# Weight loads sorted by the event that frees each buffer, a new order of expert steps, and the front part in the same Block

## What is computed

```python
xn = rmsnorm(h, g_mix); proj = xn @ w_in            # q, k, v, compressed and selected keys, gates
y_a = dilated_attention(...); y_b = nsa_attention(...)
merged = sigmoid(g_a) * (y_a @ w_branch_a) + sigmoid(g_b) * (y_b @ w_branch_b)
h = h + merged @ w_out
h = h + moe_ffn(rmsnorm(h, g_ffn))                  # 64 experts, top 8 per token, and a shared expert
h = h + (p @ w_ple) * sigmoid(rmsnorm(h, g_ple) @ w_ple_gate)
out = rmsnorm(h, g_final)
```

## Time and profile before

| | us |
|---|---|
| median of 3 runs (1224.35 to 1226.53) | 1225.8 |
| the profiled execution | 1225.4 |
| its span, first to last instruction | 1223.6 |
| PE busy | 1124.3 (92%) |
| DVE / ACT / POOL busy | 474.1 / 275.7 / 284.8 |
| mean share of the 16 DMA engines, whole span | 65% |
| DMA in all | 306.20 MB, mean 250 GB/s |

### The profile page before, as it was taken

The page is one execution under the profiler, slowest core; times in us unless marked ns, Lnnn a source line. Parts: engine busy times, 40 slices in busy tenths (PEclk is TensorE's granted clock), DMA queues, the critical chain, the costliest instruction groups (busy, mean ns, idle before and its releaser), DMA issues.

```text
span 1223.6 us, 19017 instructions
## 1 busy us (share of the span) xinstructions
PE 1124.3 (92%) x7561; PEld 657.0 (54%) x7562; DVE 474.1 (39%) x1044; ACT 275.7 (23%) x634; POOL 284.8 (23%) x212
## 2 busy tenths in 40 slices
PE   4999999999997989988999998989899897989796
PEld 3887787767765879554433343334333343323274
DVE  5335555545445743553225211212111121111786
ACT  3113333333335320010111111111111111111623
POOL 5532534343233430000111111111111111110032
PEclk8999999999997989979999998999999999989898
DMA  9821222211113203647689999999999999999771
GB/s 281 236 69 36 55 68 70 53 52 53 53 53 121 86 28 121 282 178 323 254 304 424 423 424 412 418 412 423 396 413 421 388 424 404 402 424 359 292 309 69
DMA packets 118040, 306.20 MB, mean 250 GB/s; under 512 B 21792, under 2 KB 79808, under 8 KB 91968
## 3 DMA queue, kind: packets, MB, share of 16 engines
q1 hardware_dynamic: 105712, 270.88, 57.9%
q0 software_dynamic: 12240, 34.09, 7.0%
HBM read 289.21 MB, written 26.21 MB: 258 GB/s over the span
## 4 chain that ended last, share of the span: by engine, by line
PE 37%; DMA 20%; issue 6%; SPq 2%; DVE 1%; POOLq 1%; POOL 1%; ACT 0%; DVEq 0%
DMA sb_gate_up<-in_w_up 20%; PE bank L1431 15%; PE bank L1455 7%; PE bank L1055 4%; PE bank L1043 4%; PE bank L1080 2%; PE bank L1421 2%; PE bank L1024 1%; SPq L971 1%; DMA sb_xg<-xn_rows,sb_work 1%; PE bank L1074 1%; POOLq L1782 1%; POOL sb_small L1785 1%; SPq L1471 1%; PE bank L928 0%
## 5 line engine op out<-in xcount | busy, mean ns | idle before, releaser
L1431 PE MATMUL bank<-sb_gate_up,sb_xgT 128*32 128x512 f32 (+2 forms) x2144 | 312.9, 621 | 35.8 <-DMA sb_gate_up<-in_w_up 35.8
L1431 PEld LDWEIGHTS bank<-sb_gate_up,sb_xgT 128*32 128x32 f32 (+2 forms) x2144 | 99.2, 121 | 217.9 <-issue 215.1
L457 PE MATMUL bank<-sb_x_hl,sb_w_hl 128*128 128x512 f32 x768 | 201.3, 406 | 0.0
L457 PEld LDWEIGHTS bank<-sb_x_hl,sb_w_hl 128*128 128x128 f32 x768 | 138.6, 190 | 43.8 <-issue 16.0
L1504 POOL DMA_INDIRECT expert_rows<-sb_rows_out,sb_work x42 | 43.2, 1029 | 479.7 <-DVE sb_rows_out L1576 459.9
L1455 PE MATMUL bank<-sb_down,sb_work 128*32 128x512 f32 (+2 forms) x1072 | 153.0, 595 | 1.5 <-ACT sb_work L1628 0.6
L241 POOL TENSOR_TENSOR sb_w_hl<-sb_r,sb_w_hl 128x1024 fp32r<-128x1024 f32 x54 | 132.0, 2449 | 65.6 <-ACT sb_w_hl L1163 52.9
L1586 DVE TENSOR_TENSOR sb_work<-sb_work,bank 128x256 f32<-128x256 f32 x42 | 17.8, 423 | 300.1 <-ACT sb_work L1622 300.1
L1622 ACT ACTIVATE sb_work<-bank 128x256 f32<-128x256 f32 x42 | 16.2, 386 | 327.4 <-PE bank L1431 327.4
L1455 PEld LDWEIGHTS bank<-sb_down,sb_work 128*32 128x32 f32 (+2 forms) x1072 | 47.2, 116 | 75.7 <-issue 71.9
L235 POOL CAST sb_w_hl<-sb_r 128x1024 fp32r<-128x1024 f32 x35 | 37.7, 1077 | 205.5 <-PE bank L457 158.1
(11 more groups left out here) (250 smaller groups left out, 1270.6 us busy)
## 6 DMA issues: line engine op xcount, KB each, us to landing
sb_gate_up<-in_w_gate SPq DMA_DIRECT2D x64, 1024.0 KB, 17.1
sb_gate_up<-in_w_up SPq DMA_DIRECT2D x64, 1024.0 KB, 24.0
sb_down<-in_w_down SPq DMA_DIRECT2D x64, 1024.0 KB, 21.3
sb_r<-in_w_in SPq DMA_DIRECT2D x34, 512.0 KB, 3.9
sb_rows<-expert_rows SPq DMA_DIRECT2D x6, 2048.0 KB, 16.2
sb_r<-in_w_out SPq DMA_DIRECT2D x8, 512.0 KB, 3.7
sb_rows<-expert_rows SPq DMA_DIRECT2D x4, 1024.0 KB, 7.8
sb_h<-in_x SPq DMA_DIRECT2D x4, 512.0 KB, 8.2
```

Of the source, the lines that this page charges most:

```text
L457: last = nc.tensor.matmul(out[:, :], w6_hl[:, slot_at[n], zw, k, :], x_hl[:, zx, k, :], start=k + i == 0, stop=k == KD - 1 and i == 2)
L1431: last = nc.tensor.matmul(bank[BH][rows, :], xgT[:, k, rows], gate_up[slot_of[r]][:, :, k, :], start=k == 0, stop=k == KD - 1)
```

## The change

The functions of the front become `front_sync`, `front_gpsimd`, `front_tensor`, `front_vector` and `front_scalar`, unchanged inside, and are called at the head of the second Block; the first Block is gone. ACT gets one wait ahead of the sigmoids. The order of steps is written as a string of units. The loads of the weights go to the buffer that is free first, and SP's list of loads is sorted by the event that frees the part they go to. The buffers that the tail uses are named by the last six experts instead of by fixed numbers.

```diff
-        with nc.Block() as block:
-            @block.sync
-            def _(sp):
+        def front_sync(sp):
...
-        steps = [full(r) for r in range(NPRE)]
-        next_small = NFULL + 2 * NTRIO
-        pairs_at, full_at = (0, 2, 4, 5, 7, 9, 11, 12), {3: 3, 6: 4, 10: 5}
-        for g in range(NTRIO):
-            if g in pairs_at:
+        UNITS = "FPFPFTPTTPTFTPTTPTFTPTTPTFTT"
+        steps, n_full, n_trio, next_small = [], 0, 0, NFULL + 2 * NTRIO
+        for u in UNITS:
+            if u == "F":
+                steps.append(full(n_full))
+                n_full += 1
+            elif u == "P":
                 steps.append(pair_of(next_small, next_small + 1))
                 next_small += 2
-            if g in full_at:
-                steps.append(full(full_at[g]))
-            steps += trio(NFULL + 2 * g, NFULL + 2 * g + 1, next_small)
+            else:
+                steps += trio(NFULL + 2 * n_trio, NFULL + 2 * n_trio + 1, next_small)
+                n_trio += 1
...
-        nth = {r: x for x, r in enumerate(ranks_in_order)}
-        slot_of = {r: nth[r] % NSLOT for r in ranks_in_order}
-        landed_at = {r: 16 * (nth[r] // NSLOT) + 16 for r in ranks_in_order}
+        load_order = list(range(NPRE)) + sorted((r for r in first_step if r >= NPRE), key=lambda r: (first_step[r], steps[first_step[r]].index([v for v in steps[first_step[r]] if v[0] == r][0])))
+        BUFFER = 1,2,0,3,4,5
+        slot_of, landed_at, before, holder = {}, {}, {}, {}
+        for x, r in enumerate(load_order):
+            v = x if x < NSLOT else min(holder, key=lambda i: (last_step[holder[i]], i))
+            if v in holder:
+                before[r] = holder[v]
+            landed_at[r] = 16 + (landed_at[before[r]] if r in before else 0)
+            slot_of[r], holder[v] = BUFFER[v], r
+        loads = sorted([(last_step[before[r]], 0, x, "gate_up") for x, r in enumerate(load_order) if r in before]
+                       + [(last_step[before[r]] + 1, 1, x, "down") for x, r in enumerate(load_order) if r in before])
...
             round_piece(WM_PIECE + 5)
+            act.wait_ge(F["evicted"], NF)
             for m in range(4):
                 gate(m)
...
         def experts_sync(sp):
...
+            sp.wait_ge(M["stored"], 16 * NT)
+            sp.wait_ge(M["xt_done"], NT)
+            sp.wait_ge(E["oh"], 1)
+            for x in range(NPRE, NSLOT):
+                number(x)
+                load_gate_up(sp, expert[x], load_order[x])
+                load_down(sp, expert[x], load_order[x])
+            for _, _, x, what in loads:
+                r = load_order[x]
+                if what == "gate_up":
+                    number(x)
+                    sp.wait_ge(E["gu"], last_step[before[r]] + 1)
+                    load_gate_up(sp, expert[x], r)
+                else:
+                    sp.wait_ge(E["dn"], last_step[before[r]] + 1)
+                    load_down(sp, expert[x], r)
...
             def _(sp):
+                front_sync(sp)
                 middle_sync(sp)
                 experts_sync(sp)
```

More of the change, by code:

```diff
@@ new lines, in front_scalar, with round_first, exps, copies @@
+        def front_scalar(act):
+            def round_first(n):
+                act.wait_ge(s_rawp[buf_of[n]], landed[n])
+                if freed_by[n] >= 0:
+                    act.wait_ge(F["done"], read_by[freed_by[n]])
+                nc.scalar.copy(w6_hl[:, slot_at[n], 0], raw_at[buf_of[n]]).then_inc(s_w_hi, 1)
+            for n in range(2):
+                round_first(n)
+            for k in range(KD):
+                act.wait_ge(s_tp, k + 1)
+                nc.scalar.copy(x_hl[:, 0, k, :], bank[k][:, :]).then_inc(s_hi, 1)
+            act.wait_ge(s_gn, 16)
+            nc.scalar.copy(gn_hl[:, 0], gn_w).then_inc(s_hg, 1)
+            for n in range(2, N_ACT_HI):
+                round_first(n)
+            act.wait_ge(s_hg, 3)
+            nc.scalar.activation(gates, psv(BT[0], NT, 24), ACT.Sigmoid).then_inc(s_hg, 1)
+            for i in range(2):
+                act.wait_ge(s_hid, i + 1)
+                act.wait_ge(s_w2, 80)
+                for c in range(2):
+                    nc.scalar.activation(hTc[:, i, c, :], bank[BV[i]][:, c * 64:c * 64 + 2 * NC], ACT.Gelu_apprx_tanh,
+                                         bias=b1c[:, 2 * i + c:2 * i + c + 1]).then_inc(s_gelu, 1)
+            def exps(i):
+                u = units[i]
+                if u["br"] == 0:
+                    act.wait_ge(s_c, u["pair"] - 3)
+                    for hh in range(2):
+                        nc.scalar.activation(sc[:, i % 3, hh, 0:NT * NC], sc[:, i % 3, hh, 0:NT * NC], ACT.Exp, scale=-1.0).then_inc(F["exped"], 1)
+                    return
+                for hh in range(2):
+                    act.wait_ge(F["biased"], 2 * i + hh + 1)
+                    nc.scalar.activation(sc[:, i % 3, hh, 0:n_of(u)], sc[:, i % 3, hh, 0:n_of(u)], ACT.Exp, scale=-1.0,
+                                         bias=minus_max[:, i % 4, hh:hh + 1], accum_out=rowsum[:, i % 4, hh:hh + 1]).then_inc(F["exped"], 1)
+            def copies(i):
+                u = units[i]
+                if i >= 2:
+                    act.wait_ge(F["values"], i - 1)
+                for hh in range(2):
+                    act.wait_ge(F["transposed"], 2 * i + hh + 1)
+                    rows, n = (slice(0, NC), S) if u["br"] == 0 else (slice(0, P), n_of(u))
+                    nc.scalar.copy(pT[rows, i % 2, hh, 0:n], bank[BT[hh]][rows, 0:n]).then_inc(F["copied"], 1)
+            exps(0)
+            exps(1)
+            for i in range(NU):
+                if i + 2 < NU:
+                    exps(i + 2)
+                copies(i)
+                if i >= 2 and units[i - 2]["pair"] != units[i - 1]["pair"]:
+                    p_ = units[i - 2]["pair"]
+                    act.wait_ge(F["values"], last_unit[p_] + 1)
+                    nc.scalar.copy(yT[:, p_, :], bank[BV[p_ % 2]][:, :]).then_inc(F["y_out"], 1)
+            act.wait_ge(F["done"], NF)
+            for k in range(KD - 1):
+                nc.scalar.copy(x_hl[:, 0, k, :], yT[:, k, :]).then_inc(s_yhi, 1)
+            act.wait_ge(F["values"], NU)
+            nc.scalar.copy(yT[:, 7, :], bank[BV[1]][:, :]).then_inc(F["y_out"], 1)
+            nc.scalar.copy(x_hl[:, 0, 7, :], bank[BV[1]][:, :]).then_inc(s_yhi, 1)
@@ L1379, in tables_of_rows @@
             dve.drain()
-        emb = sb("emb", R0, [P, NT, D])
-        x3 = [sb(f"x3_{b}", o, [P, 2, KD, P], F32R) for b, o in enumerate((R0 + 4096, G0))]
-        sigt = [sb("sig_ple0", G0 + 2048, [P, D]), sb("sig_ple1", place["mdil"][0], [P, D])]
-        early = sb("ple_early", G0, [P, 4, D])
+        last6 = [slot_of[r] for r in load_order[-6:]]
+        assert sorted([last6[0], last6[1], last6[4]]) == [2, 4, 5]
+        gu6, down6 = [gu_at[v] for v in last6], [down_at[v] for v in last6]
+        emb = sb("emb", gu6[5], [P, NT, D])
+        x3 = [sb(f"x3_{b}", o, [P, 2, KD, P], F32R) for b, o in enumerate((down6[5], gu6[0]))]
+        sigt = [sb("sig_ple0", gu6[0] + 2048, [P, D]), sb("sig_ple1", place["mdil"][0], [P, D])]
+        early = sb("ple_early", gu6[0], [P, 4, D])
         prow = early[:, 0, :].rearrange("p (t n) -> p t n", t=NT)
@@ L1958, in _ @@
             def _(pe):
+                front_tensor(pe)
                 middle_tensor(pe)
```

802 lines of the change are left out of this document (361 added, 441 removed).

## The result

| | us | ratio to before, 95% interval |
|---|---|---|
| before, median of 4 runs (1224.35 to 1228.04) | 1226.16 | |
| changed, median of 4 runs (1202.26 to 1205.76) | 1205.15 | 0.9824 (0.9802 to 0.9846) |
| changed, its profiled execution (span 1203.0) | 1204.86 | |

A forecast was written before the change was run, and what follows sets the result against it. PE was taken to set the pace in the first expert steps and full DMA engines later. 1225.4 - 6.5 - 18.6 + 1.0 = 1201.3, or 1201.7 us against the median; range 1194 to 1213.

The forecast's parts named there:

- What bounds the kernel: Experts: PE sets the pace in the first steps, full DMA later; early idle transfer is paid later, 26.3 us.
- Rival B: Experts and tail: all 26.3 us come back and the tail costs nothing, 1192.6 us; chance 0.08.
- rival D: Front-middle boundary: the Block does not matter, PE waits for something else at 382.6, total 1207.8 us; chance 0.05.
- Part 1: Front-middle boundary: the same Block removes 4.1 us idle and 2.4 us of half clock, 6.5 us; low case 3.0.
- The middle then is a chain of PE and DVE and moves as a whole: Middle, after the merge products: it shifts earlier unchanged, with 0 us difference forecast up to the first gate-up group.
- Part 2: Expert stage: new step order and sorted loads end it 18.6 us earlier, bounds 8.7 and 26.3.
- The recurrence: Expert stage: weight-queue ledger carried through 42 steps; ends before at 1140.7, changed at 1122.1; trusted to 3 us.
- The order of steps alone gives 8.7 us: Expert stage: new step order without sorted loads saves 8.7 us; sorted loads alone save 13.3.
- Rival A: Experts: early transfers help little, as DMA idles later instead; only 8.7 us stay, 1211.2 us; chance 0.12.
- Part 3: Tail: its 6.3 MB of loads land later, g_final 4 us after the stage; costs 1 us, bounds 0 and 3.
- Rival C: Experts: slower, waits for down weights take over; at 1.5 us later per step the kernel ends at 1262; chance 0.05.
- Early signs: Early steps over 370 GB/s, gate-up waits 20 to 28 us, down waits 3 to 12, stage end near 1113.

The follow-up runs named there:

- by event early and in turn later: Changed kernel with loads x = 6 to 13 sorted by freeing event, those from x = 14 on alternating gate-up and down: 1213.21 us, ratio 0.9909.
- the third order: Changed kernel with steps FPTTTTTFPPTPFPTTTTPPTFTTFTFP and p and w_ple loaded ahead of the last five loads: 1202.12 us, ratio 0.9809.
- the front alone: Kernel before with only the front moved into the same Block, steps and loads as before: 1221.33 us, ratio 0.9963.
- kernels with late loads in turn: Changed kernel with gate-up and down loads alternating, either from x = 14 on (1213.21 us) or for all late loads (1216.58 us, ratio 0.9922).
- Both kernels with a pair first: Changed kernel with steps PFPTTPTTFPTTTPTTTTTFFFTTPPFP: 1206.22 us; the same with p and w_ple loaded ahead of the last five loads: 1204.13 us.
- the pairs-first kernel: Changed kernel with steps PFPTTPTTFPTTTPTTTTTFFFTTPPFP, p and w_ple still loaded behind all weights: 1206.22 us, ratio 0.9845.
- in turn early: Changed kernel with loads x = 6 to 13 alternating gate-up and down, all later ones sorted by freeing event: 1213.99 us, ratio 0.9897.
- the old order with sorted loads: Changed kernel with the front in its own Block and the step order of before, loads sorted, free buffer first: 1213.95 us, ratio 0.9908.

## Why the prediction came out as it did

- **What bounds the kernel.** Right. The 26.3 us read from the earlier trace rows as a debt are borne out: each kernel that moved fewer bytes in the first 69 us than the changed one had a longer stage, and in all six the time of the missing bytes gives the extra length within about 4 us. It isn't all: by event early and in turn later, as many bytes early still left the stage 9.4 us longer, and the third order, with 359 GB/s early, has a stage 5.8 us shorter. Rival B (all 26.3 us come back) fell with a stage 16.4 us shorter, and rival D (the Block does not matter) with merge products that follow the front at once.
- **Part 1, the boundary: right in size.** 6.5 forecast, 6.2 to 6.4 in the profiles, idle time and half clock both, and no idle time of ACT or PE shows for ACT's new wait. The timing of the front alone gives less, 4.5 us. By the rule of the Trainium skill (TensorE: Matmul & The Clock Gate, What's actually happening), that activity lifts the slow state, it should be the upper value. The trace agrees here: 192 products in 43.8 us at a granted clock of 1.00. In the middle it does not agree as simply: PE was busy for all of a stretch at 0.50 (last section).
- **"The middle then is a chain of PE and DVE and moves as a whole": this step failed, by 1.9 us.** The work is the same, but the clock isn't. The low stretches at 528.0 and 545.0 in the profile of before last 6.8 us each, those at 521.7 and 538.8 in the changed kernel 10.2 each. It came back in its second profile and in three of its variants (126.6 to 126.9 us from the merge products to step 0), while in the front alone and in both kernels with late loads in turn the stretches were 6.8 us and the time 124.8 to 125.2. Both kernels with a pair first have 6.8 too, and their 127.2 and 127.3 hold some 2.5 us of waiting for the weights of step 0. What goes with the length is where on the same work the stretch falls: counted from the end of the merge products, the first one begins after 94.8 to 95.0 us in all five profiles with 10.2, and after 95.2 to 96.2 in all nine with 6.8. What sets that place isn't shown.
- **Part 2, the stage: right mechanism, 2.2 us too much.** The recurrence has 564.6 us for the changed stage, where the profiles have 564.3 and 562.6. The miss is in its figure for before, 583.2 instead of 580.7, the error that the prediction had named. The waits are near what it said: 21.9 us at the gate-up (24 forecast) and 4.9 at the down products (8 forecast). They fell by 9.0 us in all (35.8 to 26.8), which is not yet 16.4. The stretches at 0.50 within the stage add up to 27.3 us instead of 37.5, worth at most half of the difference, 5.1 us; the other 2.3 are in neither. The recurrence took 1.7 us for a gate-up group behind a long wait, where the row that it names gives 9.27 - 7.07 = 2.2.
- **"The order of steps alone gives 8.7 us": wrong, and the wrong end of the range hung on it.** That recurrence had loaded the experts in order of use, but the first three ranks are loaded ahead of the router whatever the order is. Rank 2 then holds a buffer until step 4, and in-turn loads by x mod 6 stand behind it: 15 us slower. The two halves of part 2 are not two gains that overlap, as the text had it; the new order works only with the new loads. Rival A's price, taken from the 8.7, was unfounded too, though its time (1211) stayed plausible.
- **Part 3, the tail's loads.** 1 us forecast, none seen in the changed kernel: the slack of DVE fell from 1.45 to 0.70 us and the tail took 85.2 us. But the place where such loads hurt was missed. It is not the tail but the transposes at L1565, within the last step; they waited 5.2 us in the pairs-first kernel, 3.1 in turn early and 1.1 in the old order with sorted loads.
- **Rival C.** The down wait came, at 5 us, and did not take over. The two kernels with late loads in turn have none of it and are slower. In turn early it grew to 11.3 us, the largest here, and that kernel is about as slow as they are.
- **Early signs.** Of those listed, the GB/s of the first steps came (over 370 forecast, 377 in the window that was named), and so did both ranges of waits. The stage ended at 1117.8 instead of near 1113, by the 1.9 us of clock, the 0.4 us of the front and the 2.2 us of the stage.

## What to carry to other kernels

Where one queue issues loads into buffers that come free by several events, write its list in the order of those events, and give each load the buffer that is free first; a load that waits for a late event stops all behind it. Price it by stage with a ledger of the queue, bytes against release times: idle transfer time early in a stage that is later bound by bytes came back here at about one for one. And carry in the ledger every load and every consumer on the path, those of the next stage too, and check that the variant whose price is quoted can be built.

## What was not expected of the hardware

The clock stayed at 0.50 while PE worked without a pause. In the changed kernel PE is busy for all 10.20 us of the first low stretch of the middle, with small products of the router's lists first and the shared expert's 128x512 products behind them:

```profile
521.70:531.90 10.20, 10.20 (x30) 6.77 (x30) 8.51 (x21) 0.00 (x0) 0.00 (x0) 0.50 0.00 0
```

In the kernel before, the stretch over the same kinds of products is 6.80 us, all of it busy too:

```profile
528.00:534.80 6.80, 6.80 (x25) 5.44 (x24) 5.80 (x12) 0.00 (x0) 0.00 (x0) 0.50 0.00 0
```

The shared expert's 16 products there took 9.72 us instead of 8.17, and its 8 down products, in the second low stretch, 6.11 instead of 5.44. The same work can thus cost some 2 us more or less by where a low stretch falls on it, which is as much as many changes to this kernel bring.
